# The weight sums of the first two pairs of blocks, at the program's begin: on GpSimd in place of VectorE

## What is computed

```python
for i in range(DEPTH):                       # DEPTH = 2
    h_res = h_res + 0.5 * swiglu(rms_norm(h_res, ffn1_norm[i]), ffn1_w_in[i], ffn1_w_out[i])
    h = rms_norm(h_res, mix_norm[i])
    proj = h @ w_in[i]
    ...                                      # convolution branch, attention branch, gates
    h_res = h_res + merged @ w_out[i]
    h_res = h_res + 0.5 * swiglu(rms_norm(h_res, ffn2_norm[i]), ffn2_w_in[i], ffn2_w_out[i])
# swiglu(h, w_in, w_out) = (silu(h @ w_in[:, :2816]) * (h @ w_in[:, 2816:])) @ w_out
```

## Time and profile before

| | us |
|---|---|
| median of 3 runs | 2333.5 |
| lowest, highest | 2332.78, 2334.3 |
| the profiled execution | 2333.69 |
| its span in the trace | 2331.9 |
| busy in it: TensorE matmuls | 2308.5 |
| VectorE | 1676.5 |
| ScalarE | 1245.2 |
| GpSimd | 324.5 |

### The profile page before, as it was taken

The page is one execution under the profiler, slowest core; times in us unless marked ns, Lnnn a source line. Parts: engine busy times, 40 slices in busy tenths (PEclk is TensorE's granted clock), DMA queues, the critical chain, the costliest instruction groups (busy, mean ns, idle before and its releaser), DMA issues.

```text
span 2331.9 us, 43089 instructions
## 1 busy us (share of the span) xinstructions
PE 2308.5 (99%) x17685; PEld 2202.1 (94%) x17685; DVE 1676.5 (72%) x2761; ACT 1245.2 (53%) x2029; POOL 324.5 (14%) x424
## 2 busy tenths in 40 slices
PE   7999999999999999999999999999999999999999
PEld 6999999999999999999999999999888787998997
DVE  7855754798896588567788557548998865874863
ACT  8734733554455477357567347334545455762751
POOL 1100101211211111011011011011212202110110
PEclk9999999999999999999999999999999999999999
DMA  6855836777676768468458457367777657773853
GB/s 188 183 129 137 177 90 147 151 166 151 149 147 164 170 143 185 112 147 185 116 132 182 129 134 178 90 150 156 160 167 154 152 162 175 166 179 103 180 126 110
DMA packets 109347, 351.09 MB, mean 151 GB/s; under 512 B 12384, under 2 KB 12384, under 8 KB 109152
## 3 DMA queue, kind: packets, MB, share of 16 engines
q0 software_dynamic: 59760, 194.54, 41.5%
q1 hardware_dynamic: 49024, 153.47, 22.4%
q10 hardware_dynamic: 368, 0.33, 0.0%
HBM read 343.80 MB, written 2.10 MB: 148 GB/s over the span
## 4 chain that ended last, share of the span: by engine, by line
PE 93%; DVE 2%; DMA 1%; issue 1%; ACT 1%; DVEq 0%; POOL 0%; ACTq 0%
PE po L1169 33%; PE po L1186 23%; PE po L1237 22%; PE ptr L1186 7%; PE pov L1186 5%; PE pstat L1385 1%; PE pov L1424 1%; PE pov L1427 1%; DMA wla<-in_mixes 1%; DMA wha<-in_mixes 1%; PE ptr L1394 1%; DVE rms L1666 0%; DVE wla L1593 0%; PE pstat L1350 0%; ACT whb L716 0%
## 5 line engine op out<-in xcount | busy, mean ns | idle before, releaser
L1169 PE MATMUL po<-xh,wha 128*128 128x264 f32 (+1 forms) x1408 | 344.3, 311 | 0.0
L1169 PE MATMUL po<-xl,wha 128*128 128x264 f32 (+1 forms) x1408 | 335.5, 305 | 0.0
L1169 PE MATMUL po<-xh,wla 128*128 128x264 f32 (+1 forms) x1408 | 334.8, 304 | 0.0
L1834 DVE SCALAR_TENSOR_TENSOR cv<-ub,lp,cv 128x528 f32<-128x528 f32 (+1 forms) x480 | 333.1, 751 | 1.7
L1237 PE MATMUL po<-hh,wla 128*128 128x264 f32 (+1 forms) x1232 | 283.7, 300 | 0.0
L1237 PE MATMUL po<-hl,wha 128*128 128x264 f32 (+1 forms) x1232 | 283.7, 300 | 0.0
L1237 PE MATMUL po<-hh,wha 128*128 128x264 f32 (+1 forms) x1232 | 282.4, 299 | 0.0
L1601 DVE TENSOR_TENSOR wla<-wfa,wha 128x768 fp32r<-128x768 f32 (+1 forms) x128 | 113.2, 889 | 197.0 <-ACT wha L745 196.9
L1169 PEld LDWEIGHTS po<-xh,wha 128*128 128x128 f32 x1408 | 227.0, 188 | 17.6 <-issue 1.8
L745 ACT ACTIVATE wha<-wfa 128x768 fp32r<-128x768 f32 (+1 forms) x128 | 101.0, 789 | 262.1 <-DMA wfa<-in_outs 262.1
L1169 PEld LDWEIGHTS po<-xh,wla 128*128 128x128 f32 x1408 | 226.4, 188 | 11.0
(11 more groups left out here) (258 smaller groups left out, 5651.8 us busy)
## 6 DMA issues: line engine op xcount, KB each, us to landing
raw<-in_pairs SPq DMA_DIRECT2D x88, 768.0 KB, 5.3
wha<-in_mixes POOLq DMA_DIRECT2D x120, 512.0 KB, 4.3
wla<-in_mixes POOLq DMA_DIRECT2D x120, 512.0 KB, 6.6
wfa<-in_outs SPq DMA_DIRECT2D x64, 384.0 KB, 3.1
wlb<-in_pairs POOLq DMA_DIRECT2D x47, 512.0 KB, 8.3
raw<-in_pairs SPq DMA_DIRECT2D x88, 256.0 KB, 6.6
wla<-in_pairs POOLq DMA_DIRECT2D x88, 256.0 KB, 6.4
wla<-in_pairs POOLq DMA_DIRECT2D x40, 512.0 KB, 8.4
```

The source lines that it names most:

```text
L1169: ins = mm(po[:, 2 * out_slot + h, 0:width], w[:, k, :], v[:, k, t:t + width], start=begin and k == 0 and p == 0, stop=last and k == kt - ...
L1834: stt(cv[:, j, a:], u, w, cv[:, j, a:], ALU.mult, ALU.add).then_inc(conv_step, 1)
```

## The change

GpSimd gets a function `pair_sums(j)` that makes the four sums of a pair with its own additions, waiting for both loads of the pair first and, between dependent additions, for `s_sum`. It stands in GpSimd's queue before `base22_lo(0)` for pair 0 and before `base_lo(1)` for pair 1. VectorE's calls of `sum12` and `sum43` for pairs 0 and 1 go; those of the first step of later stages stay (`if s:`). All other pairs' sums stay on VectorE.

```diff
+            def pair_sums(j):
+
+                padd = lambda out_, a, b: nc.gpsimd.tensor_tensor(out=out_, in0=a, in1=b, op=ALU.add)
+                pool.wait_ge(raw_in[j % 2], 16 * (j // 2 + 1))
+                pool.wait_ge(raw22_in[j % 2], 16 * (j // 2 + 1))
+                tile4 = lambda i: raw[:, j % 2, i * KP:(i + 1) * KP, :]
+                s12 = units(f32_units, U_S12[REGION[j]], 2)
+                s43 = units(f32_units, U_S43[REGION[j]], 2)
+                padd(s12[:, 0:KP, :], tile4(0), tile4(3)).then_inc(s_sum, 1)
+                pool.wait_ge(s_sum, 4 * j + 1)
+                padd(s12[:, KP:, :], tile4(1), s12[:, 0:KP, :]).then_inc(s_sum, 1)
+                pool.wait_ge(s_sum, 4 * j + 2)
+                padd(s43[:, 0:KP, :], tile4(2), s12[:, KP:, :]).then_inc(s_sum, 1)
+                padd(s43[:, KP:, :], tile4(1), tile4(3)).then_inc(s_sum, 1)
+
+            pair_sums(0)
             base22_lo(0)
+            pair_sums(1)
             base_lo(1)
             for l in range(DEPTH):
                 stage(2 * l)
@@
                 if k == 1:
                     first_base_lo()
-                if k == 4:
-                    sum12(0)
                 if k == 5:
-                    sum43(0)
                     sum_lo(0, 0)
             sum_lo(0, 1)
 
@@
                             gate_sum(j, 0)
-                            sum12(j + 1)
-                            sum43(j + 1)
+                            if s:
+                                sum12(j + 1)
+                                sum43(j + 1)
                             if s == 0:
                                 gate_sum(j, 1)
                             rms_half(l, s, 0)
```

## The result

The changed kernel takes **2338.6 us** as the median of 8 runs (2337.71 to 2341.75), the kernel before 2333.24 (8 runs, 2331.01 to 2334.3). The ratio is 1.0026, with a 95% interval of 1.0017 to 1.0035: the change costs 5.4 us by the medians, 4.0 to 8.2 by the interval. The time lies in the range. It is not the sum that was forecast (2336.4, within 0.2% of before) but near rival B's 2338.9, slower than before by a little over 0.2% by the medians (the interval begins at 0.17%).

A forecast was written before the change was run, and what follows sets the result against it. TensorE bounds the kernel; at the begin it waits for VectorE and ScalarE. Removed additions -1.05 plus GpSimd collisions +4.0 (6 x 0.7 - 0.2) gave +2.95 on 2333.5: 2336.4 us, range 2332.2 to 2340.0.

The forecast's parts named there:

- rival B: 8.8 to 16 and 19.7 to 25 us: GpSimd holds VectorE off for its whole addition; +5.35, 2338.9 at 1.1 us; chance 0.27.
- What bounds the begin: Over 8 to 16 us VectorE and ScalarE prepare operands in turn while TensorE waits; delaying either delays the begin.
- Gain of the removed additions, -1.05: Pair 0's last two additions leaving VectorE (23.06 to 24.26 us) save about 1.05 us, capped by ScalarE's idle time.
- enough, barely: TensorE before its late products: 1.9 us left for nine P5 products (1.1) and the last tiles' statistics matmuls (some 0.6).
- Length of an addition, 1.1: One 128x512 GpSimd addition takes 1.1 us, from the select's rate and the skill's figure; bounds 0.68 and 2.3.
- c = 0.7: Each colliding GpSimd addition holds VectorE back 0.7 us, its own time to read the two tiles; total +4.0 us.
- six charged: Six GpSimd additions delay VectorE: pair 0's four and two of pair 1's; the other two fall into VectorE's free time.
- c = 1.0: Delay of VectorE per GpSimd addition from which the kernel is slower by over 0.2% (4.7 us).
- Slack, 0.2: Only some 0.2 us of VectorE's delay is free before ScalarE's x7h at 12.30 us.
- Moved transfers: Pair 1's accumulating transfer, base22 and SP's loads of pairs 2 and 3 shift; delays hidden, no gain.
- rival C: Late transfer binds: with harmless 2.3 us additions, pair 1's accumulating transfer lands too late; 2334 to 2336.6; chance 0.06.
- Rival A: The engines do not disturb one another (c = 0 to 0.2), so -1.05 stays: 2332.4; chance 0.24.

The follow-up runs named there:

- short additions: Changed kernel with GpSimd's eight additions each working on 8 of 512 columns, same queue place and waits: 2332.67 us, ratio 0.9999.
- memsets: Changed kernel with the eight GpSimd additions replaced by eight write-only memsets of 128x1024: 2332.51 us, ratio 1.0.
- the sums moved on VectorE: Kernel before with pair 0's last two additions moved directly behind its first two on VectorE, nothing on GpSimd: 2332.24 us, ratio 0.9996.
- pair 0 alone: Changed kernel with only pair 0's four additions on GpSimd, pair 1's on VectorE as before: 2336.71 us, ratio 1.0019.
- the kernel with the busy matmuls: Changed kernel with 21 additional 128x128 identity matmuls where TensorE waits for the third operand pair: 2335.24 us, ratio 1.0012.
- The last experiment: Kernel before plus five GpSimd additions of 128x512 from about 31 us on, on unused tiles: one run, 2336.64 us, time not used.
- the copies: Changed kernel with the eight GpSimd additions replaced by copies of one 128x512 tile each: 2332.86 us, ratio 1.0003.

## Why the prediction was right, and where its sum was off

- **What bounds the begin**: right. ScalarE and VectorE hand each other work, and VectorE's delay passes through. All of the change's effect is in place by 60 us.
- **Gain of the removed additions, -1.05**: right for VectorE's chain (x7l -1.0 with short additions, memsets, and the sums moved on VectorE). That TensorE had "enough, barely" cover was wrong: with its clock at half through the early products, only 0.25 to 0.3 us of the 1.0 reaches P5 of pair 1; with the clock full, all of it. One of the terms was also too small: the statistics matmuls of the last tiles, put at some 0.6 us, take 1.6 (26.39 to 27.98 with the sums earlier), so that with the 1.1 us of P5 products TensorE needs 2.7 us where the sum had 1.9 for them.
- **Length of an addition, 1.1**: 1.26 to 1.35 us where VectorE does not hold it off, 1.5 to 2.1 where it does.
- **What one costs VectorE, c = 0.7**: this term was mis-sized. Measured, 1.03 to 1.07 us for each of pair 0's four and 0.95 and 1.08 for two of pair 1's: six charged, as counted, 6.2 us in sum instead of 4.2. The reason given for 0.7, that the engines share just the time that VectorE would need for the tiles, is refuted. By the lengths, VectorE waits for almost the whole GpSimd addition, all but 0.2 to 0.3 us of its 1.26 to 1.35: rival B's mechanism, whose point of decision, c = 1.0, is passed by a little. By the rule of the Trainium skill ("SBUF — State Buffer", Who interferes with whom) a VectorE instruction with two SBUF inputs contends with a GpSimd instruction that reads SBUF, and not with one that only writes it. These runs agree: two SBUF inputs on VectorE are held, a PSUM operand or a single input is not, a GpSimd memset holds nothing, and a GpSimd copy does.
- **Slack, 0.2**: ScalarE and VectorE absorbed 0.8. 6.2 - 1.05 would be +5.2 at x7l, measured +4.4. The charged 0.2 are there: of the first three collisions (3.14 us) 2.96 arrive at ScalarE's tile at 15.15, counted from the common row. But the fourth falls in part into VectorE's own wait of 0.22 us before 12.25, and pair 0 alone, with 4.2 us of collisions, came out at +2.6, so 0.6 of the 0.8 belong to it.
- **Missing from the sum**: TensorE's clock. Its wait before the sixth tile's statistics grew from 2.48 to 3.20 us, with two more of 0.85 and 0.72 around it, and the half clock lasted until the late products; 2.0 us, which the kernel with the busy matmuls did not lose. So 4.4 + 2.0 = 6.4 us at P5 of pair 1 stand where the forecast had 2.95; the medians show 5.4.
- **Moved transfers**: right. Pair 1's accumulating transfer was issued at 26.19, landed 7.8 us later at 34.0, and nobody waited for it; rival C did not occur. Rival A is refuted by VectorE's rows.
- **What was luck**: the time lies in the range because the range took in rival B up to 1.3 us for an addition, not because the sum was right: that was 2.2 us too low in the median. And that 2338.6 comes within 0.3 us of B's 2338.9 is luck in part: B's sum had no clock in it (2.0 us) and too little slack (0.6 us), and the 6.4 us lost in the trace at P5 are 1 us more than the medians differ.

## What to carry to other kernels

An idle GpSimd is not free help for VectorE: in these runs an elementwise operation there that read SBUF cost the VectorE instruction with two SBUF inputs that it met most of its own length (1.05 of some 1.3 us for an addition, 0.4 of 0.61 for a copy), so 0.68 us taken off VectorE came back as 1.05. Such work belongs beside VectorE instructions with a PSUM operand or one input, or into time in which VectorE idles. And before work is moved to another engine, look for an idle gap on its own: here the 1.44 us behind the first two sums took the other two, with the same 1.0 us gained at x7l and at no price, though the whole time shows no gain.

## What was not expected

The half clock of TensorE is a second price of a delay at the begin: where the x7l chain was late by 2.6 and 2.9 us it cost 0.8 us more, where it was late by 4.4 it cost 2.0, and nothing with matmuls that fill the wait. It can also swallow a gain: 0.7 of 1.0 us with the sums moved earlier.

Whether it falls differs between traces in a way that the change does not set. The last experiment's kernel has the instructions of the kernel before until 30.85 us, and yet its clock over 20 to 34 us was 1.00 against 0.88, and its wait before the sixth tile 1.69 us against 2.48. With the short additions and the copies, too, the clock stayed at 1.00 without any filling, with waits of 1.24 and 1.78 us. In these three traces TensorE's first products, at 15.4 to 16.2 us, took 0.42 us each, where before they took 0.29, and so it was busy for longer ahead of the wait. That alone does not keep the clock up: with pair 0 only the first products took 0.42 us as well, the wait was 3.20 us, and the clock fell (0.88). The kernel with the busy matmuls also had slow first products and, with its wait filled, a full clock. Why the first products were slower in some traces stays open: the granted clock of those rows is 1.00, and there is one trace of each kernel. For the same reason the column "lost behind x7l" is one execution's, not a mean.
